# Two of four pooling means as band-matrix products on TensorE, and the pool projection two weight slots earlier

## The reference

```python
def causal_window_mean(u, w):
    cs = jnp.pad(jnp.cumsum(u, axis=1), ((0, 0), (1, 0), (0, 0)))
    upper = cs[:, 1:]
    lower = jnp.pad(cs, ((0, 0), (w - 1, 0), (0, 0)))[:, :S]
    count = jnp.minimum(jnp.arange(1, S + 1), w)
    return (upper - lower) / count[None, :, None]

def pool_mixer(h, w_grp, b_grp, scale):
    for gi, w in enumerate((2, 4, 8, 16)):
        u = h[..., gi * 256:(gi + 1) * 256]
        groups.append(causal_window_mean(u, w) - u)
    p = jnp.stack(groups, axis=2)
    return (einsum('bsgc,gcd->bsgd', p, w_grp) + b_grp).reshape(B, S, 1024) * scale

# every layer
x = x + 0.5 * swiglu_ffn(rmsnorm(x, n_ffn1[i]), ...)
x = x + mixer(rmsnorm(x, n_mix[i]))
x = x + mem_cross_attn(rmsnorm(x, n_xattn[i]), rmsnorm(mem, n_mem[i]), ...)
x = x + 0.5 * swiglu_ffn(rmsnorm(x, n_ffn2[i]), ...)
```

## Time and profile before

| | us |
|---|---|
| three runs | 2109.51, 2111.41, 2112.24 |
| median | 2111.41 |
| profiled execution | 2109.99, its span 2108.1 |
| PE busy | 2066.6 (98%) |
| DVE / ACT / POOL busy | 941.1 / 710.1 / 131.8 |

### The profile page before, as it was taken

How to read it: one execution, slowest core, us unless ns; L and a number is a source line. 1 busy time by engine, 2 the same in 40 slices (tenths; PEclk the granted TensorE clock), 3 DMA queues, 4 the chain that set the end, 5 groups by cost and what they waited for, 6 DMA issues and landing times.

```text
span 2108.1 us, 24613 instructions
## 1 busy us (share of the span) xinstructions
PE 2066.6 (98%) x9956; PEld 1742.0 (83%) x9956; DVE 941.1 (45%) x997; ACT 710.1 (34%) x841; POOL 131.8 (6%) x111
## 2 busy tenths in 40 slices
PE   8999999999999999999999999999987999999998
PEld 6888888799998888888888888888876888888887
DVE  4343333476455455343333443343287444343333
ACT  5222222354354443222222422232135443222222
POOL 1000001000001001000001000000064010000000
PEclk9999999998899999999999999999999999999999
DMA  5322223211123223322223222322333123322231
GB/s 161 99 88 91 95 96 109 82 60 61 60 81 120 93 88 120 99 86 93 95 96 109 98 86 95 99 95 90 96 119 104 56 80 100 99 91 90 94 110 55
DMA packets 192699, 197.10 MB, mean 93 GB/s; under 512 B 3554, under 2 KB 191072, under 8 KB 192640
## 3 DMA queue, kind: packets, MB, share of 16 engines
q1 hardware_dynamic: 191104, 192.95, 28.2%
q0 software_dynamic: 928, 2.25, 0.3%
q10 hardware_dynamic: 608, 1.06, 0.1%
HBM read 194.15 MB, written 2.10 MB: 93 GB/s over the span
## 4 chain that ended last, share of the span: by engine, by line
PE 93%; DVE 4%; ACT 2%; issue 1%; DMA 0%; ACTq 0%; DVEq 0%
PE ps L300 31%; PE ps L302 30%; PE ps L301 30%; DVE w_lo L1370 1%; ACT w_hi L962 1%; DVE h_lo L1373 0%; DVE sums L1750 0%; DVE x L1785 0%; PE ps L735 0%; DVE up L1920 0%; PE ps L794 0%; ACT p_tok L1163 0%; DMA x_tok<-in_x 0%; ACT h_hi L962 0%; PE ps L590 0%
## 5 line engine op out<-in xcount | busy, mean ns | idle before, releaser
L300 PE MATMUL ps<-h_hi,w_hi 128*128 128x512 f32 (+1 forms) x1728 | 671.1, 388 | 10.7 <-DVE w_lo L1370 6.1
L301 PE MATMUL ps<-h_lo,w_hi 128*128 128x512 f32 (+1 forms) x1728 | 667.3, 386 | 0.0
L302 PE MATMUL ps<-h_hi,w_lo 128*128 128x512 f32 (+1 forms) x1728 | 667.2, 386 | 0.0
L1370 DVE TENSOR_TENSOR w_lo<-raw,w_hi 128x2048 fp32r<-128x2048 f32 (+3 forms) x192 | 420.5, 2190 | 475.4 <-ACT w_hi L962 475.4
L962 ACT ACTIVATE w_hi<-raw 128x2048 fp32r<-128x2048 f32 (+3 forms) x192 | 346.9, 1807 | 268.4 <-PE ps L302 268.4
L300 PEld LDWEIGHTS ps<-h_hi,w_hi 128*128 128x128 f32 x1728 | 326.0, 189 | 80.0 <-issue 8.4
L302 PEld LDWEIGHTS ps<-h_hi,w_lo 128*128 128x128 f32 x1728 | 325.6, 188 | 65.8
L301 PEld LDWEIGHTS ps<-h_lo,w_hi 128*128 128x128 f32 x1728 | 325.8, 189 | 64.8 <-issue 0.7
L300 PE MATMUL ps<-mid_hi,w_hi 128*128 128x512 f32 x704 | 274.0, 389 | 0.0
L302 PE MATMUL ps<-mid_hi,w_lo 128*128 128x512 f32 x704 | 273.9, 389 | 0.0
L301 PE MATMUL ps<-mid_lo,w_hi 128*128 128x512 f32 x704 | 273.9, 389 | 0.0
(11 more groups left out here) (300 smaller groups left out, 1982.6 us busy)
## 6 DMA issues: line engine op xcount, KB each, us to landing
raw<-in_ffn_w_gu SPq DMA_DIRECT2D x87, 1024.0 KB, 5.1
raw<-in_ffn_w_down SPq DMA_DIRECT2D x32, 1024.0 KB, 4.9
raw<-in_x_w_kv SPq DMA_DIRECT2D x16, 1024.0 KB, 5.3
raw<-in_ffn_w_down SPq DMA_DIRECT2D x16, 768.0 KB, 4.3
raw<-in_gla_w_in SPq DMA_DIRECT2D x12, 1024.0 KB, 5.1
raw<-in_x_w_q SPq DMA_DIRECT2D x8, 1024.0 KB, 5.0
raw<-in_x_w_o SPq DMA_DIRECT2D x8, 1024.0 KB, 4.9
raw<-in_gla_w_out SPq DMA_DIRECT2D x8, 512.0 KB, 3.4
```

Source lines behind the costliest of these rows:

```text
L300: nc.tensor.matmul(out_ap, left[0], right[0], start=first, stop=False)
L301: nc.tensor.matmul(out_ap, left[0], right[1], start=False, stop=False)
L302: return nc.tensor.matmul(out_ap, left[1], right[0], start=False, stop=last)
L1370: return nc.vector.tensor_tensor(out_ap, value, hi.bitcast(F32), ALU.subtract)
```

## The change

POOL no longer computes means. Once the memory of layer two is transposed, in the middle of `ffn(2)`, POOL builds `band`: for windows 8 and 16 a matrix of 128 source tokens by 144 target tokens that holds 1/w on the band and less one on the diagonal, in one version for the first 128 tokens (with the true counts in the first 16 columns) and one for the others. ACT and DVE split it (`band_split`). In the mixer, PE transposes chunks 4 to 7 of x into tokens on the partitions (16 transposes), ACT and DVE scale and split them (`tokens`), and PE multiplies them with the band (`window_means`, nine matmuls for each chunk), after which ACT and DVE apply the gain and split (`window_means`). The projection with its slot moves in front of the value slots 2 and 3; the normed memory is packed into chunks 4 to 7 of `h_hi`/`h_lo`, so that `feed(6, m)` may write chunks 0 to 3 before the last value slots are read, and chunks 4 to 7 only behind them.

```diff
@@ place_rest
         for h in range(4):
+            if h == 2:
+                place("pool", 8, 8, C)
             place(("xv", 1, h), 2, 2, C)
-        place("pool", 8, 8, C)
@@ regions
-        mem_norm = ((m_hi, m_lo), (h_hi, h_lo))
+        mem_norm = ((m_hi, m_lo), tuple(h[:, C // 2:, :].rearrange("p a (b n) -> p (a b) n", n=MEM) for h in (h_hi, h_lo)))
@@ gpsimd
-            def pool_last_groups():
...
+            def bands():
+                pool.wait_ge(sig.mem_transposed, 2 * C)
+                pool.wait_ge(sig.counts_ready, 7)
...
-            for f in (4, 5):
-                add_squares(f)
-            pool_last_groups()
+            add_squares(4)
+            bands()
+            add_squares(5)
@@ tensor
+            def transpose_tokens(tt):
...
+                if tt == 2:
+                    pe.wait_ge(sig.tok_ready, TOK_FEEDS.index(5) + 1)
+                if tt == 3:
+                    pe.wait_ge(sig.xt_lo_ready, 1)
+                for n in range(4):
+                    last = nc.tensor.transpose(ps[:, bank, n * P:(n + 1) * P], x[:, 4 + n, tt * P:(tt + 1) * P], ident[:])
...
+            def window_means(m):
...
+                pe.wait_ge(sig.band_lo_ready, 1)
+                pe.wait_ge(sig.xt_lo_ready, T)
+                if m == 5:
+                    pe.wait_ge(sig.norm_ready, RMS_FEEDS.index(5) + 1)
+                for tt in range(T):
+                    hi, lo = xt_hi[:, g, tt, ms], xt_lo[:, g, tt, ms]
+                    n = min(BAND, SEQ - tt * P)
+                    to = ps[:, bank, tt * P:tt * P + n]
+                    if tt == 0:
+                        nc.tensor.matmul(ps[:, bank, :], hi, first_hi[:, g, :], start=True, stop=False)
+                        nc.tensor.matmul(to, lo, first_hi[:, g, 0:BAND], start=False, stop=False)
+                        nc.tensor.matmul(ps[:, bank, 0:PAD], hi, first_lo[:, g, :], start=False, stop=False)
+                    else:
+                        nc.tensor.matmul(to, hi, later_hi[:, g, 0:n], start=False, stop=False)
+                        last = nc.tensor.matmul(to, lo, later_hi[:, g, 0:n], start=False, stop=tt == T - 1)
...
             norm(5)
+            transpose_tokens(0)
+            transpose_tokens(1)
             cross_keys(1, (1,))
             spread_rms(5)
-            cross_keys(1, (2, 3))
-            for h in range(4):
-                project_rows(("xv", 1, h), mem_norm[1], MT)
+            transpose_tokens(2)
+            transpose_tokens(3)
+            cross_keys(1, (2,))
+            window_means(4)
+            window_means(5)
+            cross_keys(1, (3,))
+            window_means(6)
+            window_means(7)
+            project_rows(("xv", 1, 0), mem_norm[1], MT)
+            project_rows(("xv", 1, 1), mem_norm[1], MT)
+            project_pool()
+            project_rows(("xv", 1, 2), mem_norm[1], MT)
+            project_rows(("xv", 1, 3), mem_norm[1], MT)
@@ scalar
-            for m in range(4, C):
-                hi_part(up[:, m, PAD:], x[:, m, :], scale=gain(5, m)).then_inc(sig.up_gained, 1)
...
+            for m in range(0, C, 2):
+                pool_output(m)
+                pool_output(m + 1)
+                feed(6, m // 2)
             split_next(at["pool"].slot)
+            feed_square(6, 4)
+            feed_square(6, 5)
+            cross_values(1, 2)
+            feed_square(6, 6)
+            feed_square(6, 7)
+            cross_values(1, 3, split=False)
+            for m in range(4, C):
+                feed_hi(6, m)
+            split_next(at[("xv", 1, 3)].slot)
```

More of the change, by code:

```diff
@@ L237, in trunk @@
         probs_T = ((pT_hi, pT_lo), (pT_odd_hi, pT_odd_lo))
[L239 to L243, removed]
+        up = region("up", 0, [P, 4, PAD + SEQ])
+        sums = region("sums", 8 * KB + 512, [P, 2, 2, PAD + SEQ])
+        means = (sums[:, 0], sums[:, 1])
+        p_hi, p_lo = region("p_hi", 72 * KB, [P, 4, SEQ], F32R), region("p_lo", 80 * KB, [P, 4, SEQ], F32R)
+        BAND = P + PAD
+        xt_hi, xt_lo = region("xt_hi", 17 * KB, [P, 2, T, 2 * P], F32R), region("xt_lo", 25 * KB, [P, 2, T, 2 * P], F32R)
+        pt_hi, pt_lo = region("pt_hi", 17 * KB, [P, 4, SEQ], F32R), region("pt_lo", 25 * KB, [P, 4, SEQ], F32R)
+        band = region("band", 88 * KB, [P, 2, 2, BAND])
+        first_hi = region("first_hi", 90 * KB + 512, [P, 2, SEQ], F32R)
+        later_hi = region("later_hi", 94 * KB + 512, [P, 2, BAND], F32R)
+        first_lo = region("first_lo", 95 * KB + 768, [P, 2, PAD], F32R)
         y_tok = region("y_tok", 0, [P, T, D])
@@ L355, in load_cross_values @@
                 for h in range(4):
+                    if (i, h) == (1, 2):
+                        w = at["pool"].slot
+                        load(w, w - 1, C, io.pool_w[0].rearrange("g (k p) n -> p (g k) n", p=P))
                     load_fixed(("xv", i, h), io.x_w_kv[i], 0, C, D + h * COLS)
@@ new lines, in project_pool @@
+            def project_pool():
+                w = at["pool"].slot
+                pe.wait_ge(sig.w_lo_ready, w + 1)
+                for g in range(4):
+                    if g < 2:
+                        pe.wait_ge(sig.p_lo_ready, g + 1)
+                    else:
+                        pe.wait_ge(sig.pt_lo_ready, 2 * g - 2)
+                    hi, lo = ((p_hi, p_lo), (pt_hi, pt_lo))[g // 2]
+                    for c in range(2):
+                        bank = chunk_bank(at["pool"].out + 2 * g + c)
+                        for kk in range(2):
+                            at_p = 2 * (g % 2) + kk
+                            last = three_products(ps[:, bank, :], weights(w % 2, 2 * g + kk, c),
+                                                  (hi[:, at_p, :], lo[:, at_p, :]), kk == 0, kk == 1)
+                        last.then_inc(sig.part_done, 1)
@@ L1667, in cross_values @@
                                    xv_lo[:, mt, vs], xv_hi[:, mt, vs])
-                split_next(at[("xv", i, h)].slot)
+                if split:
+                    split_next(at[("xv", i, h)].slot)
             def cross_outputs(i, h):
```

181 lines of the change are left out of this document (100 added, 81 removed).

## The result

| | before | changed |
|---|---|---|
| median of four runs each, us | 2110.46 (2108.68 to 2112.24) | 2092.64 (2092.58 to 2092.94) |
| ratio | | 0.9916, interval 0.9899 to 0.9933 |
| profiled execution, us | 2109.99 | 2092.58 |
| span, us | 2108.1 | 2090.8 |

A forecast was written before the change was run, and what follows sets the result against it. PE, busy 98% of the span, was taken as the bound. 25.5 - 6.5 - 1.4 - 4.1 - 1.7 = 11.8, called 12 us, took the profiled 2109.99 to 2098.0; adding 1.42 gave 2099.4 us, range 2095 to 2106.

The forecast's parts named there:

- What goes: Layer two's mixer, second key to second query slot: PE's 20.4 us of waits and 5.1 of low clock vanish, 25.5.
- PE's work: Layer two's mixer: 16 transposes at 1.6 us and 36 band matmuls at 4.9 add 6.5 us to PE's path.
- The first new wait: Projection's second group: PE waits 1.0 us for `p_lo` and 0.4 for an evacuation; bounds 0 and 3.
- The second: Last value slot: PE waits 4.1 us for its split, queued behind DVE's and ACT's other work; bounds 2.3 and 5.5.
- The clock: After the last value slot's wait: 3.4 us at half clock, charged once at 1.7 us; bounds 0 and 3.4.
- the third rival: Last value slot: wait only 2.3 us with no fall of the clock, 3.5 us more gain, 2096 us; chance 15%.
- Clock at the short matmuls: Transposes and band matmuls: PE's clock falls twice there, costing 3.4 us, 2102.8 us; chance 15%.
- DVE late all the same: Five weight slots: DVE late by 1 us each, plus another clock fall, gives back 6 to 7 us, 2106; chance 10%.
- Small new waits: Last value slot: ACT alone sets the split, wait 2.3 us, no clock fall, 2096 us; chance 15%.
- Dear bands: Down projection: slow band selections on POOL delay ACT's weight split, eating the gain or reaching 2119 us; chance 3%.

The follow-up runs named there:

- n1: The kernel before with POOL's means of groups three and four left out, POOL only writing zeros there: 2092.15 us, ratio 0.9907.
- o1: The kernel before with the projection ahead of the last two value slots and the memory packed as in the change, means still on POOL: 2109.49 us, ratio 0.9986.
- m1: The changed kernel with the projection put back behind all four value slots: 2093.76 us, ratio 0.9915.
- a1: The changed kernel, unaltered, run once more for a third profile: 2092.16 us in one profiled run.
- b0: The kernel before, unaltered, run again for another profile: 2110.61 us, ratio 0.9996.
- a0: The changed kernel, unaltered, run again beside its variants: 2092.86 us, ratio 0.9918.
- b1: The kernel before, unaltered, run once more for a third profile: 2112.53 us in one profiled run.
- d1: The changed kernel with every band product computed twice, 72 matmuls in place of 36: 2097.81 us, ratio 0.9938.
- s1: The changed kernel with the last value slot's split ahead of the projection's last two outputs on ACT and DVE: 2092.82 us, ratio 0.9912.
- k1: The changed kernel with the squares of chunks 0 to 3 moved behind the last value slot's split, on ACT: 2092.14 us, ratio 0.9912.
- s2: The changed kernel with both the last value slot's split early and the squares of chunks 0 to 3 late: 2092.85 us, ratio 0.9914.

## Why the prediction missed

The mechanism was right: POOL's means held DVE up, DVE's splits held PE up, and both ended with them (n1, o1, m1). Its own steps, in the profiled pair, where the stretch became 92.14 - 76.50 = 15.6 us shorter and 11.8 had been worked out:

- **What goes.** I had 25.5 us: the waits and the low clock of before. a1 has no low clock in the stretch, so its length without what is charged apart is 75.06 - 6.0 - 0.9 - 2.55 = 65.6, and before lost 92.14 - 65.6 = 26.5: 1.0 more. Of that, 0.28 is an eighth wait, for `p_lo` in the projection, that the sum left out; the rest isn't traced to a row.
- **PE's work.** 0.83 + 0.79 us of transposes and 2.21 + 2.19 of bands are 6.0 instead of 6.5. The nine took 1.08 us where I had 1.2. The 0.125 us for a short matmul came from one of 256 columns; with 16 to 144 columns it is nearer to 0.11.
- **The first new wait.** 0.89 instead of 1.4; the evacuation behind `p_lo` ended it, not `p_lo`.
- **The second.** 2.55 instead of 4.1, near my lower bound. DVE began its twelve instructions 2.5 us earlier than I had it, but so did PE (1.6 us by the start of the stretch, the rest by the two items above), which leaves the wait as it is. They took 1589.65 - 1577.91 = 11.7 us, where I had 12.6; and the split, which I had end at about 1596, 3.0 us behind them, took 2.28, since POOL was the one that gave way. That is 0.9 + 0.7 = 1.6 us. The 11.7 us hold 1.06 us of waits for ACT's outputs (0.19, 0.44 and 0.43) that my sum of durations hadn't, so the instructions themselves were 1.9 us shorter than I had them: fewer of them were slowed by POOL.
- **The clock.** I charged 1.7 us once. Two profiles of three show the fall of 3.4 us behind the last value slot, at a price of 1.45 us (the last value slot takes 7.30 us with it and 5.85 without); one shows none.

These sum to 1.0 + 0.5 + 0.5 + 1.55 + 0.25 = 3.8 us. Another 1.6 us lie ahead of the change: the stretch starts at 1534.51 instead of 1536.12. That is chance: the first mixer had 3.4 us less low clock in this execution (see b0), and in six profiles these starts are 1536.12, 1536.57 and 1536.15 before and 1534.51, 1537.08 and 1535.60 in the changed kernel. Behind the stretch both take 479.8 us.

**The step that failed** is the sum, in the size of its terms; in the profiled pair the largest error of one is the wait at the last value slot, put at 4.1 us and measured at 2.55. It was too long because I let POOL's squares slow four of DVE's twelve instructions and the split behind them as well; they slowed fewer, and the split not at all. Over three profiles each, which averages the clock, before's stretch is 92.69 and the changed one's 76.02, 16.7 us apart where I had worked out 11.8. The missing 4.9 us are 1.6 in what goes (27.1 instead of 25.5), 0.5 in PE's work, 0.5 in the first wait, 1.55 in the second and 0.7 in the clock.

**A second error** is the last line of the sum, "the median of the runs shown is 1.42 above it, so 2099.4". I carried before's distance between its profile and its median over to the changed kernel, and it isn't a constant: with a fourth run before's median is 2110.46 and the distance 0.47; the changed kernel's profile and median are 2092.58 and 2092.64; and in a0 the profile is 2.4 us above the median. A part of before's distance may be the very low clock that the change removes, since nearly the same waits came with 17 us of low clock in one profile of before and with more in b1, whose stretch is 1.5 us longer and whose time 2.5; that isn't shown. The 6.8 us between 2099.4 and the profiled 2092.58 are so 3.8 from the sizes, 1.6 from chance and 1.4 from this line. The profiled executions lie on average at 2111.04 and 2093.32, 17.7 apart, as the medians are (17.8).

**The range** failed by how it was made. I had bounds for PE's work, for both waits and for the clock behind them, but let only the last wait and its clock give: the lower end, 2095, is the third rival with 1 us below it. With all low bounds together 25.5 - 5.7 - 0 - 2.3 - 0 = 17.5 us are gained, which is 2092.5 from the profile and 2093.9 with the 1.42 added. There was no bound for the low clock of before or for the start, which move by 1.5 us and more from profile to profile.

**One row was misread.** DVE is full in all three windows of the earlier trace rows (3.33 of 3.40 us in the first), not in two. The argument gets stronger by it and no number changes.

**The rivals.** Clock at the short matmuls: false, also at twice the length (d1). DVE late all the same: false, 2.29 us a split up to the projection. Small new waits, 2096: the nearest, with 2.55 us for its 2.3, and in a1 and d1 without a fall. Its reason wasn't the one: ACT alone was to set the split, and DVE's chain still did (the split follows the last `h_lo` with no wait for ACT, though ACT's `w_hi` was ready only 0.2 us earlier, at 1589.53). Dear bands: false; ACT waited 2.6 us for them and PE nothing. My 0.29 us for a selection was low for the first four (3.13 / 4 = 0.78) and right for the last four (0.27).

What stays open: that PE still waits 1.74 and 1.00 us for `w_lo` at two value slots of n1, while in m1, with 6.0 us more on PE, only 0.87 are left, I read as PE's added work filling those gaps; it wasn't tested with a filler of another kind. And why s1, k1 and s2 shorten the stretch by 2.5 to 3.2 us against a0 (1.1 to 1.8 against a1) and the medians don't move is settled only in part.

## What to carry to other kernels

When two engines share work out of the same SBUF, look at what the helper costs the engine it helps: POOL's 43 us were idle time used, and cost PE 19 us through DVE (n1's stretch against before's). A matrix engine that is waiting can take 6 us of short products for less than their length (1.7 us between the stretches of m1 and n1, about 3.4 at equal clock), so moving work onto the bound engine may pay, if it removes what the engine waits for. A forecast should be built from median to median or from profile to profile, and a distance between them, which changed from 1.42 to 0.47 us with one more run, shouldn't be carried over to another kernel. When a sum has five uncertain terms, the range should let more than one of them be wrong.

## What the runs showed of the hardware

- Who starts first keeps its time. Before, DVE's split began at 1589.36, behind POOL's subtraction at 1587.77, and took 3.77 us, to 2.1 us behind POOL's end at 1590.99. In the changed kernel the split at 1589.65 began first and took its 2.28 us, and POOL's addition at 1590.12 took 2.96, to 1.1 us behind the split's end; beside the next split it was 2.30 and 3.16. Both losers look as if they had begun when the other ended. The Trainium skill (SBUF — State Buffer, "Who interferes with whom") says that the order of issue decides who blocks, not the shape of the operation; the trace agrees. It is also why the loser has to be looked for on POOL: there ACT's next square waited 2.67 us for it.
- The same wait doesn't always lower the clock. 2.55 us at the same place did in two profiles and not in a third (nor did 2.53 in d1). 2.4 us at the queries' first matmuls did in b1 and n1 and not in before or b0. The 2.49 us wait of the earlier trace rows was followed by low clock there and in b0 by none (mean 1.00 from 1680 to 1690). A 1.15 us wait did lower it in s2. Short matmuls in pieces of 2.2 and 4.4 us left it at 1.00, though in the first mixer it had fallen among short matmuls.
- A matmul with 16 to 144 columns costs 0.06 to 0.15 us start to start; nine matmuls, one of them of 512 columns, cost 1.08 us.
